# First-layer FFNs: gate/value pairs as seven half products instead of eight, and the second matrix in two passes

## The chip, the core and the metric

The kernel runs on one core of a Trainium2 chip. The time is the device time of one execution in microseconds (us), as the median of the runs shown. It multiplies in fp32 through TensorE: each operand is split into a high part that TensorE takes in one pass (fp32r) and a low part, the rest, and a product is three matmuls: high x high, low weight x high, high weight x low.

## The reference

Two "first" layers and two "second" layers on a sequence of 512 tokens, 1024 channels. A first layer has a SwiGLU FFN, a group of mixers, and a second SwiGLU FFN, each behind an RMS norm with a shift, scale and gate that come from a condition vector:

```python
def adaln_pre(h, g, shift, scale):
    return rms_norm(h, g) * (1 + scale) + shift

def swiglu(h, w13, w2):              # w13: 1024 x (2 * 2816), w2: 2816 x 1024
    a, b = jnp.split(h @ w13, 2, axis=-1)
    return (jax.nn.silu(a) * b) @ w2
```

The change is to `swiglu` in the first layers alone: 2 layers with 2 FFNs each, 4 in all.

## The kernel before

Activations lie channel by token: `xT` is 8 tiles of 128 channels x 512 tokens, `hH`/`hL` the split output of the norm, `gH`/`gL` the split gated product, 22 tiles of 128x512. A weight unit is 128 output channels with all their input tiles, 128x1024 (8 k tiles) in the first matrix and 128x1408 (11 k tiles, half of a column) in the second. A unit goes from `wR` (raw, by DMA on SyncE's queue) through ScalarE, which writes the high part `wH` (a copy that rounds, L1119), and VectorE, which writes the low part `wL = wR - wH` (L1687). There are two buffers, and a third one (`third`) for the openings.

An FFN is an opening, a loop and a second matrix:

- The norm works in two halves of 256 tokens. VectorE makes `hf` (L1822), ScalarE rounds it to `hH` (L1222), VectorE makes `hL` (L1828). Meanwhile `open_three` (PE, L2895) multiplies the first three units k by k in halves of 256 columns, and the fourth unit follows with 512.
- `up` (PE, L2927): the other 20 pairs of a gate and a value unit, each unit 8 k x 3 matmuls of 512 columns (`products`, L2890 to L2892). For each pair ScalarE takes the silu of the gate out of PSUM (L1169), VectorE multiplies it with the value (L1716), rounds (L1718) and takes the low part (L1720). In most pairs VectorE also makes two dots of 128x1024 against `cond` (L1662), for the shift, scale and gate of later norms; their weights `adaw` come by DMA.
- `down` (PE, L2949): 8 tiles of 22 k x 3 matmuls. VectorE adds each to `xT` with its gate (L1753); GpSimd squares it and adds up the squares for the next norm (`square_sum`, L2698 and L2701). The last tile is done in two halves of 256 columns (`last`, L2964 to L2966), and the mean square (L3008, L3011) is put between, so that root and norm of the next opening run beside the rest of it.

The order of each engine's instructions is written out by hand, with semaphores between engines (`w_hi`, `w_lo`, `w_used`, `sil`, `g_mul`, `x_new`). SyncE issues all DMAs in one order. In layer 0 the opening also holds the tables of the position bias: four matmuls and copies, and 32 small copies of GpSimd (`compressed_bias`, L2788).

## Time and profile before

| | |
|---|---|
| median of 3 runs | 3521.57 us (3520.69 to 3525.12) |
| span of the profiled execution | 3521.1 us |
| TensorE busy | 3406.2 us, 97% |
| TensorE weight loads | 2804.2 us, 80% |
| VectorE | 1994.7 us, 57% |
| ScalarE | 1164.4 us, 33% |
| GpSimd | 333.0 us, 9% |
| DMA | 386.77 MB, mean 110 GB/s |

All times are from one profiled execution, taken next to the runs; its span is 0.5 us below their median. In the lists a line is a line of the kernel, `PE` is TensorE's matmuls, `DVE` VectorE, `ACT` ScalarE, `POOL` GpSimd. `out<-in` names tiles without buffer numbers. A matmul's length in the timeline holds its way through the array, so back-to-back matmuls overlap: their rate is read from their starts.

### The profile page before, as it was taken

The page shows a single profiled execution, that of the slowest core. Times are in us where ns is not written, and L with a number is a line of the kernel's source. Part 1 is how long each engine was busy: PE and PEld are TensorE (multiplying, and loading weights), DVE is VectorE, ACT ScalarE, POOL GpSimd, SP SyncE. Part 2 cuts the span into 40 slices and gives each one's busy share as a digit, 9 for nine tenths or more (in the row PEclk, how much of TensorE's full clock was granted, in tenths as well). Part 3 has the DMA queues.
Part 4 walks back from the last instruction along what each step waited for, and adds up shares of the span by engine and source line. Part 5 has one row for each costly group of instructions (what it writes and reads, how often), then busy time and mean ns, then how long its engine had stood idle before and what let it go on. Part 6 is the DMA issues. An engine that isn't in the chain of part 4 may idle for free.

```text
span 3521.1 us, 49654 instructions
## 1 busy us (share of the span) xinstructions
PE 3406.2 (97%) x18508; PEld 2804.2 (80%) x18508; DVE 1994.7 (57%) x3164; ACT 1164.4 (33%) x1766; POOL 333.0 (9%) x293
## 2 busy tenths in 40 slices
PE   7999999989999999999998999999999999999999
PEld 6888877678888888887777888887788888688887
DVE  6763447666653566345766765446666625766642
ACT  4222334433221322234443322233443314443321
POOL 0000100141000000010014100011200011120002
PEclk9999999989999999999998999999999999999999
DMA  7653222103543355322210354321222332123232
GB/s 295 219 191 102 91 78 85 42 11 133 195 141 106 118 194 195 109 93 84 84 42 11 129 191 144 107 94 60 76 80 96 105 104 73 55 80 99 95 104 82
DMA packets 100835, 386.77 MB, mean 110 GB/s; under 512 B 11134, under 2 KB 12286, under 8 KB 99800
## 3 DMA queue, kind: packets, MB, share of 16 engines
q1 hardware_dynamic: 100696, 384.82, 32.0%
q8 instruction: 99, 1.62, 0.2%
q14 instruction: 40, 0.33, 0.0%
HBM read 382.65 MB, written 2.12 MB: 109 GB/s over the span
## 4 chain that ended last, share of the span: by engine, by line
PE 87%; DVE 7%; ACT 3%; issue 1%; DMA 1%; POOL 0%; SPq 0%; ACTq 0%; DVEq 0%; POOLq 0%
PE bank L2890 18%; PE bank L2892 18%; PE bank L2891 18%; PE bank L3016 4%; PE bank L3018 4%; PE bank L3017 4%; PE bank L2901 1%; PE bank L2902 1%; PE bank L2903 1%; PE bank L2966 1%; PE bank L2965 1%; PE bank L2964 1%; PE bank L3104 1%; PE bank L3627 1%; PE bank L3628 1%
## 5 line engine op out<-in xcount | busy, mean ns | idle before, releaser
L1119 ACT ACTIVATE wH<-wR 128x1024 fp32r<-128x1024 f32 (+2 forms) x378 | 428.9, 1135 | 1393.7 <-PE bank L2892 1305.5
L1687 DVE TENSOR_TENSOR wL<-wR,wH 128x1024 fp32r<-128x1024 f32 (+2 forms) x384 | 509.3, 1326 | 595.5 <-ACT wH L1119 591.0
L2890 PE MATMUL bank<-hH,wH 128*128 128x512 f32 x1920 | 747.8, 389 | 4.1 <-DVE wL L1687 4.1
L2892 PE MATMUL bank<-hL,wH 128*128 128x512 f32 x1920 | 747.6, 389 | 0.0
L2891 PE MATMUL bank<-hH,wL 128*128 128x512 f32 x1920 | 747.5, 389 | 0.0
L2890 PEld LDWEIGHTS bank<-hH,wH 128*128 128x128 f32 x1920 | 360.8, 188 | 79.7 <-DVE wL L1687 5.0
L2891 PEld LDWEIGHTS bank<-hH,wL 128*128 128x128 f32 x1920 | 360.8, 188 | 75.2
L2892 PEld LDWEIGHTS bank<-hL,wH 128*128 128x128 f32 x1920 | 360.6, 188 | 75.0
L2890 PE MATMUL bank<-gH,wH 128*128 128x512 f32 x924 | 359.4, 389 | 0.0
L2891 PE MATMUL bank<-gH,wL 128*128 128x512 f32 x924 | 359.4, 389 | 0.0
L2892 PE MATMUL bank<-gL,wH 128*128 128x512 f32 x924 | 359.4, 389 | 0.0
L3016 PE MATMUL bank<-hH,wH 128*128 128x512 f32 x672 | 285.8, 425 | 0.0
L3018 PE MATMUL bank<-hL,wH 128*128 128x512 f32 x672 | 266.2, 396 | 0.0
L3017 PE MATMUL bank<-hH,wL 128*128 128x512 f32 x672 | 265.3, 395 | 0.0
L2636 DVE SCALAR_TENSOR_TENSOR xn<-bank,par,xn 128x511 f32<-128x511 f32 (+1 forms) x176 | 131.5, 747 | 127.1 <-ACT xn L1604 115.7
L2891 PEld LDWEIGHTS bank<-gH,wL 128*128 128x128 f32 x924 | 173.4, 188 | 36.1
L2890 PEld LDWEIGHTS bank<-gH,wH 128*128 128x128 f32 x924 | 173.4, 188 | 36.1
L2892 PEld LDWEIGHTS bank<-gL,wH 128*128 128x128 f32 x924 | 173.4, 188 | 35.9
L1716 DVE TENSOR_TENSOR gf<-bank,sil 128x512 f32<-128x512 f32 x88 | 60.8, 691 | 244.9 <-PE bank L2892 241.8
L1662 DVE CUSTOM_DVE_ANT_0 adaw<-adaw,cond 128x1024 f32<-128x1024 f32 x144 | 170.3, 1220 | 0.0
L3016 PEld LDWEIGHTS bank<-hH,wH 128*128 128x128 f32 x672 | 128.3, 191 | 43.1 <-issue 20.6
L2698 POOL TENSOR_TENSOR sumsq<-xT 128x512 f32<-128x512 f32 x8 | 8.3, 1042 | 1611.6 <-DVE xT L1753 1582.7
(496 smaller groups left out, 5254.9 us busy)
## 6 DMA issues: line engine op xcount, KB each, us to landing
wR<-in_ffn_w SPq DMA_DIRECT2D x176, 512.0 KB, 3.4
adaw<-in_ada_w SPq DMA_DIRECT2D x144, 512.0 KB, 5.3
wR<-in_ffn_w SPq DMA_DIRECT2D x64, 704.0 KB, 4.0
wR<-in_w_up SPq DMA_DIRECT2D x88, 512.0 KB, 3.3
wR<-in_w_mix SPq DMA_DIRECT2D x76, 512.0 KB, 3.3
wR<-in_w_down SPq DMA_DIRECT2D x32, 704.0 KB, 4.0
wR<-in_w_in SPq DMA_DIRECT2D x40, 512.0 KB, 3.3
wR<-in_w_out SPq DMA_DIRECT2D x16, 512.0 KB, 3.3
```

Of the source, the lines that this page charges most:

```text
L1119: act.activation(wH[n][:, 0:tiles, :], wR[n][:, 0:tiles, :], ACT.Copy).then_inc(S.w_hi, 1)
L1662: return dve.tensor_tensor_reduce(w, w, cond[:, :], 1.0, 0.0, ALU.mult, ALU.add, dst)
L1687: dve.tensor_tensor(wL[n][:, 0:tiles, :], wR[n][:, 0:tiles, :], wH[n][:, 0:tiles, :].bitcast(F32), ALU.subtract).then_inc(S.w_lo, 1)
L1716: dve.tensor_tensor(gf[:, :], bank[b][:, :], sil[:, :], ALU.mult).then_inc(S.g_mul, 1)
L2636: dve.scalar_tensor_tensor(y, bank[b][:, 0:T - d], par[:, bass.ds(E_CW + 3 * (i + FT * half) + 2 - d, 1)], y, ALU.mult, ALU.add).then_inc( ...
L2890: pe.matmul(o, wH[n][:, k, :], rH[:, r, :], start=start and k == 0, stop=False)
L2891: pe.matmul(o, wL[n][:, k, :], rH[:, r, :], start=False, stop=False)
L2892: mm = pe.matmul(o, wH[n][:, k, :], rL[:, r, :], start=False, stop=stop and k == tiles - 1)
L2901: pe.matmul(o, wh[:, k, :], hH[:, k, c], start=k == 0, stop=False)
L3016: pe.matmul(o, wH[n][:, k, :], hH[:, k, :], start=k == 0, stop=False)
L3017: pe.matmul(o, wL[n][:, k, :], hH[:, k, :], start=False, stop=False)
L3018: mm = pe.matmul(o, wH[n][:, k, :], hL[:, k, :], start=False, stop=k == KT - 1)
```

## The change

In each first-layer FFN the first two gate/value pairs stay as they were. The other 20 are made one pair at a time as one product of a 2x2 block matrix. The weights of a pair are four blocks of 128 outputs x 512 inputs (gate or value, inputs 0 to 511 or 512 to 1023), h is four blocks of 512 inputs x 256 tokens. Eight block products become seven (Strassen, in Winograd's form), with sums of blocks ahead and sums of products behind:

- Weights: a pair comes as one DMA of 128x2048 (`RW`, two buffers). GpSimd makes four sums of 128x512 (`sums`). ScalarE rounds and VectorE takes low parts in three groups: 128x1536 (three raw blocks), 128x1024 and 128x1024 (the sums). The groups have one buffer each (`slots`), and group i of the next pair is written when its last product of this pair is done.
- h: the norm keeps its unrounded halves (`HB`, `wide`), GpSimd makes four block sums of 128x1024 once per FFN (`block_sum`), ScalarE and VectorE split them.
- Products: P1, P2, P4, P5, P6, P3, P7, each 4 k x 3 matmuls of 256 columns, each to a PSUM bank of its own (`turn`).
- Results: ScalarE copies P1 out of PSUM, VectorE makes seven sums of 128x256, each of one PSUM bank and one SBUF tile (`total`). ScalarE takes the silu of both halves, GpSimd multiplies with the value (`gated`, two of 128x256), ScalarE rounds, GpSimd takes the low part (`g_low`, 128x512).

The sums need space, so gated tiles are kept for half of the columns only (`gHc`, `gLc`, 11 tiles). The FFN runs in two chunks: 2 direct + 9 pairs, a pass of the second matrix over 11 k with its result added to `xT` (`x_mid`), then 11 pairs and a second pass over the other 11 k. In `down` a unit was half a column of the second matrix; it is now a tile of one pass, with an add to `xT` after each. The last tile is halved in the second pass only; the mean square stands 5 k into its second half, with 6 k behind it.

The dots are spread anew: one dot per turn for turns 1 to 8 of chunk A, in a layer's first FFN also for turns 1 to 10 of chunk B, the rest two by two in the passes of the second matrix. The dots of the first gate of layer 0, which had loads of their own, come in this stream. In layer 0 `compressed_bias` stands behind GpSimd's first sums and block sums and ahead of the sums of the turns. Semaphores of other parts are merged, with no change of order there. The numbers of the weights' layout on the host change to match.

The diff, cut to the turns and what feeds them:

```diff
+            # ScalarE
+            def chunk(f, q0, q1, u, half):
+                for q in range(q0, q1 + 1):
+                    keep_p1(f, q)
+                    if q > q0:
+                        g_high(f, q - 1)
+                    act.wait_ge(S.q_v, of(S.q_v, f, 7, n_sum("a_lo", q)))
+                    act.activation(sil[:, 0:W2], sil[:, 0:W2], ACT.Silu).then_inc(S.q_s, 1)
+                    act.wait_ge(S.q_p, of(S.q_p, f, 7, n_mult(4, q)))
+                    if q < q1:
+                        raw_in(f, q + 1)
+                        group1(f, q + 1)
+                        act.wait_ge(S.q_p, of(S.q_p, f, 7, n_mult(6, q)))
+                        group2(f, q + 1)
...
+                    act.wait_ge(S.q_v, of(S.q_v, f, 7, n_sum("a_hi", q)))
+                    act.activation(sil[:, W2:T], sil[:, W2:T], ACT.Silu).then_inc(S.q_s, 1)
+                    if q < q1:
+                        act.wait_ge(S.q_p, of(S.q_p, f, 7, n_mult(7, q)))
+                        group3(f, q + 1)
...
+            # VectorE
+            def chunk(f, q0, q1, u, half, c=None):
+                for q in range(q0, q1 + 1):
+                    dve.wait_ge(S.q_c, of(S.q_c, f, 1, q + 1))
+                    if q:
+                        dve.wait_ge(S.q_g, of(S.q_g, f, 2, 2 * q))
+                    total(f, q, "a_lo", 2, p1s, sil[:, 0:W2])
+                    if c is not None and q > q0 and q - q0 <= (10 if half else 8):
+                        dot(c + (q - q0 - 1) // 2, (q - q0 - 1) % 2)
+                    if q < q1:
+                        group1(f, q + 1)
...
+                    total(f, q, "u2", 6, p1s, u2s)
+                    summed(f, q, "u2")
+                    total(f, q, "x4", 4, u2s, x4s[:, :])
+                    total(f, q, "v", 5, u2s, vs[:, :])
+                    summed(f, q, "v")
+                    total(f, q, "a_hi", 3, vs[:, :], sil[:, W2:T])
+                    if q < q1:
+                        group2(f, q + 1)
+                    dve.wait_ge(S.g_lo, at(S.g_lo, FT * f + q + 2))
+                    total(f, q, "b_hi", 7, vs[:, :], gf[:, W2:T])
+                    total(f, q, "b_lo", 7, x4s[:, :], gf[:, 0:W2])
+                    if q < q1:
+                        group3(f, q + 1)
...
+            # GpSimd
+                    out, x, y, op = ((sA[:, 0:TT, :], a21, a22, ALU.add), (sA[:, TT:w, :], sA[:, 0:TT, :], a11, ALU.subtract),
+                                     (sB[:, 0:TT, :], a12, sA[:, TT:w, :], ALU.subtract), (sB[:, TT:w, :], a11, a21, ALU.subtract))[i]
...
+                    for q in range(q0, q1 + 1):
+                        if q > q0:
+                            gated(q - 1)
+                        if q < q1:
+                            pool.wait_ge(S.q_lo, of(S.q_lo, f, 3, 3 * q + 2))
+                            sums(q + 1, 0)
+                        if q > q0:
+                            g_low(q - 1)
+                        if q < q1:
+                            sums(q + 1, 1)
+                            pool.wait_ge(S.q_lo, of(S.q_lo, f, 3, 3 * q + 3))
+                            sums(q + 1, 2)
+                            sums(q + 1, 3)
...
+            # TensorE
+            def product(o, w, bh, bl):
+                wh, wl = w
+                for k in range(TT):
+                    pe.matmul(o, wh[:, k, :], bh(k), start=k == 0, stop=False)
+                    pe.matmul(o, wl[:, k, :], bh(k), start=False, stop=False)
+                    mm = pe.matmul(o, wh[:, k, :], bl(k), start=False, stop=k == TT - 1)
+                mm.then_inc(S.q_p, 1)
```

## Rows read from the trace of the kernel before

**Rows 1.** The page, part 4: shares of the chain that ended last
```profile
PE 87%; DVE 7%; ACT 3%; issue 1%; DMA 1%; POOL 0%; SPq 0%; ACTq 0%; DVEq 0%; POOLq 0%
```
**Rows 2.** Stretch table, first-layer FFN: stretch, length, busy us per engine, granted clock, DMA
```profile
850.00:1200.00 350.00, 350.00 (x1628) 293.45 (x1627) 167.36 (x228) 83.30 (x92) 15.92 (x13) 1.00 0.42 146
```
**Rows 3.** Timeline, TensorE, 512 columns: start, length, engine, line, operation (54 steps)
```profile
899.75 0.39 PE L2890 MATMUL bank<-hH,wH 128*128 128x512 f32 x1
...
911.99 0.39 PE L2890 MATMUL bank<-hH,wH 128*128 128x512 f32 x1
```
**Rows 4.** Timeline, TensorE, 256 columns, last tile of an FFN (86 steps)
```profile
395.81 0.28 PE L2964 MATMUL bank<-gH,wH 128*128 128x256 f32 x1
...
406.13 0.28 PE L2966 MATMUL bank<-gL,wH 128*128 128x256 f32 x1
```
**Rows 5.** Timeline, VectorE, two 128x1024 low parts back to back
```profile
36.49 1.22 DVE L1770 TENSOR_TENSOR third<-wR,third 128x1024 fp32r<-128x1024 f32 x1
37.63 1.22 DVE L1770 TENSOR_TENSOR wL<-wR,wH 128x1024 fp32r<-128x1024 f32 x1
```
**Rows 6.** Groups by shape, VectorE: count, busy us, mean ns, idle before
```profile
L1687 DVE TENSOR_TENSOR wL<-wR,wH 128x1024 fp32r<-128x1024 f32 x278 | 341.7, 1229 | 130.5 <-ACT wH L1119 125.9 <-ACT wH L1144 4.3 <-DVE gate L2368 0.2
...
L1716 DVE TENSOR_TENSOR gf<-bank,sil 128x512 f32<-128x512 f32 x88 | 60.8, 691 | 244.9 <-PE bank L2892 241.8 <-PE bank L2924 3.2
```
**Rows 7.** Groups by shape, GpSimd
```profile
L2830 POOL TENSOR_TENSOR pm<-pm,COS 128x512 f32<-128x512 f32 x16 | 20.6, 1285 | 151.1 <-PE bank L3565 151.1
...
L2727 POOL TENSOR_TENSOR hf<-pm 128x512 f32<-128x512 f32 x8 | 8.3, 1042 | 205.2 <-DVE pm L2157 205.2
...
L2751 POOL TENSOR_TENSOR OQ<-OD 128x1024 f32<-128x1024 f32 x2 | 3.8, 1895 | 80.3 <-ACT OD L1411 80.3
```
**Rows 8.** Groups by shape, ScalarE
```profile
L1119 ACT ACTIVATE wH<-wR 128x1024 fp32r<-128x1024 f32 x272 | 287.8, 1058 | 825.7 <-PE bank L2892 755.7 <-PE bank L3018 28.5 <-PE bank L2924 13.3
```
**Rows 9.** DMA issues: tile, queue, count, KB each, median us to landing
```profile
adag<-in_ada_first SPq DMA_DIRECT2D x3, 1024.0 KB, 7.3
```
**Rows 10.** Timeline, GpSimd and VectorE where both read two SBUF tiles
```profile
704.97 0.67 DVE L2218 TENSOR_TENSOR PP<-NN,LM 128x512 f32<-128x512 f32 x1
...
705.39 3.04 POOL L2769 TENSOR_TENSOR TMP<-NN,LM 128x512 f32<-128x512 f32 x2
...
705.67 1.64 DVE L2221 SCALAR_TENSOR_TENSOR PP<-PP,cst 128x512 f32<-128x512 f32 x1
...
707.23 1.75 DVE L2218 TENSOR_TENSOR PP<-NN,LM 128x512 f32<-128x512 f32 x1
```
**Rows 11.** Timeline, the same on a 128x1024 low part, and on a PSUM input
```profile
2548.95 1.22 DVE L1770 TENSOR_TENSOR third<-wR,third 128x1024 fp32r<-128x1024 f32 x1
...
2549.18 1.89 POOL L2698 TENSOR_TENSOR rstd<-xT 128x512 f32<-128x512 f32 x1 [5.31 <-DVE xT L2623]
...
2551.14 1.30 POOL L2701 TENSOR_TENSOR sumsq<-sumsq,rstd 128x512 f32<-128x512 f32 x1
...
2551.43 0.75 DVE L2623 SCALAR_TENSOR_TENSOR xT<-bank,gate,xT 128x512 f32<-128x512 f32 x1 [1.27 <-PE bank L3629]
```
**Rows 12.** Timeline, opening of an FFN: norm's second half, fifth unit
```profile
841.72 0.87 DVE L1822 SCALAR_TENSOR_TENSOR hf<-xT,modA,rstd 128x256 f32<-128x256 f32 x2
...
858.95 0.39 PE L2890 MATMUL bank<-hH,wH 128*128 128x512 f32 x1
```
**Rows 13.** Timeline, GpSimd: the compressed bias of layer 0
```profile
63.07 5.44 POOL L2788 COPY cb<-cskew 128x16 f32<-128x16 f32 x32 [62.63 <-DMA cskew<-bias_by_distance_up]
```
**Rows 14.** Timeline, TensorE: mean square, and first matmul of the next opening
```profile
406.25 0.60 PE L3008 MATMUL bank<-sumsq,cst 128*128 128x256 f32 x2
...
411.07 0.28 PE L2901 MATMUL bank<-hH,third 128*128 128x256 f32 x1
```
**Rows 15.** Stretch table, TensorE alone in the mixers: busy us (count), granted clock, DMA
```profile
728.00:736.00 8.00, 7.21 (x222) 1.00 0.01 2
704.00:712.00 8.00, 3.14 (x12) 0.64 0.00 0
```

More of the change, by code:

```diff
@@ L566, in build, with weights @@
         gL = place("gL", [P, FT, T], F32R)
+        o_wr = top[0]
         wR = [place(f"wR{i}", [P, KH, P]) for i in range(2)]
-        wH = [place(f"wH{i}", [P, KH, P], F32R) for i in range(2)]
-        wL = [place(f"wL{i}", [P, KH, P], F32R) for i in range(2)]
+        WT = 4 * P
+        w_hl = [place(f"w{n}", [P, 31, P], F32R) for n in ("H", "L")]
+        def weights(tile, tiles):
+            return [w[:, tile:tile + tiles, :] for w in w_hl]
+        wH, wL = zip(weights(0, KH), weights(12, KH))
+        third = weights(23, KT)
+        tail = weights(20, KH)
+        slots = [weights(4 * i, TT) for i in range(7)]
+        G1 = weights(0, 3 * TT)
+        G2 = weights(12, 2 * TT)
+        G3 = weights(20, 2 * TT)
         o_ex = [top[0]]
@@ L573, in build @@
         YC = place("YC", [P, 2, H * HD])
-        third = [place(f"third{i}", [P, KT, P], F32R) for i in range(2)]
         W3 = ((wH[0], wL[0]), (wH[1], wL[1]), third)
@@ L1052, in stream_ada @@
-                with sp.Fori(3 if start else 1, turns // 2) as i:
-                    for e in range(2):
-                        turn(2 * i + e, e, True)
-                with sp.Fori(turns, FT - 1) as i:
-                    turn(i, 0, False)
-                turn(FT - 1, 0, False)
+                sp.wait_ge(S.h_lo, at(S.h_lo, 2 * KT * (n + 1)))
+                sp.wait_ge(S.t_s, at(S.t_s, 4 * f + 4))
+                pair(f, 1, wq, l)
+                columns(c, l, False)
+                c += 1
@@ new lines, in columns, with group1, group2 @@
+            def columns(c):
+                for j in range(2):
+                    dot(c, j)
+            def group1(f, q):
+                dve.wait_ge(S.q_hi, of(S.q_hi, f, 3, 3 * q + 1))
+                dve.tensor_tensor(G1[1], RW[kind(q)][:, 0:3 * TT, :], G1[0].bitcast(F32), ALU.subtract).then_inc(S.q_lo, 1)
+            def group2(f, q):
+                dve.wait_ge(S.q_hi, of(S.q_hi, f, 3, 3 * q + 2))
+                dve.tensor_tensor(G2[1], sA[:, :, :], G2[0].bitcast(F32), ALU.subtract).then_inc(S.q_lo, 1)
@@ L1743, in up @@
-                with dve.Fori(4 if start else 1, turns // 2) as i:
-                    for e in range(2):
-                        turn(2 * i + e, KT)
-                        columns(2 * i + e, e)
-                dve.wait_ge(S.ada_done, at(S.ada_done, done + turns))
-                with dve.Fori(turns, FT - 1) as i:
-                    turn(i, KT)
-                turn(FT - 1, next_tiles)
-            def add_to_x(m, b, sub):
+                    dve.wait_ge(S.g_hi, at(S.g_hi, FT * f + i + 1))
@@ new lines, in ffn @@
+                gates()
+                for m in range(KT):
+                    if m == KT - 1:
+                        group1(f, Q_A)
+                        group2(f, Q_A)
+                        columns((ADA_DN1, ADA_DN2)[f] + m)
+                    dve.wait_ge(S.w_used, at(S.w_used, udn + m + 1))
+                    add_to_x(m, 2 + m % 2, sub, S.x_mid)
+                    if m + 2 < KT:
+                        down_low(udn, m + 2, 0)
+                    if m < KT - 1:
+                        columns((ADA_DN1, ADA_DN2)[f] + m)
@@ new lines, in ffn @@
+                group3(f, Q_A)
+                u = udn + KT
+                chunk(f, Q_A, NQ - 1, u, 1, None if f else ADA_UPB)
+                for m in range(KT - 1):
+                    dve.wait_ge(S.w_used, at(S.w_used, u + m + 1))
+                    add_to_x(m, 2 + m % 2, sub)
+                    if m + 2 < KT:
+                        down_low(u, m + 2, 1)
+                    if f == 0 and m < ADA_UP2 - ADA_FAR:
+                        columns(ADA_FAR + m)
+                    if rest and m < 4:
+                        rest(m)
@@ L2943, in up, with ffn @@
+            def ffn(f, ubase, udn, xbase, n, ss, between=None, late=False, start=False):
+                open_three(ubase, n, late, not start)
                 if between:
                     between()
-                gate_unit(1, bank[3][:, :])
-                with pe.Fori(2, FT) as i:
-                    turn(i)
+                pe.wait_ge(S.w_lo, at(S.w_lo, ubase + 4))
+                products_third(bank[3][:, :])
+                if between:
+                    pe.wait_ge(S.bm_set, H)
+                chunk(f, 0, Q_A, udn, 0, S.x_mid, KT * f)
+                chunk(f, Q_A, Q_B, udn + KT, 1, S.x_new, xbase, ss)
@@ L3476, in layer1 @@
                 warm(WARM)
-                up(U_UP2, FT, 2, late=True)
                 def next_layer():
```

731 lines of the change are left out of this document (504 added, 227 removed).

## The prediction

> **What bounds the kernel now.** First the page's chain [rows 1]: TensorE carries 87% of the chain that ended last, the next engine 7%. Then the stretch table of one first-layer FFN [rows 2]: in 850 to 1200 TensorE is busy 350.0 of 350 us at full clock, VectorE 167, ScalarE 83, GpSimd 16, and no wait of TensorE's is left to remove. So only TensorE's work counts here now, and the other engines have idle time. The question is whether they still have it when work is given to them.
>
> **What TensorE saves.** From 899.75 to 911.99 there are 54 steps between matmuls of 512 columns: 0.2267 us each [rows 3]. From 395.81 to 406.13 there are 86 steps of 256 columns: 0.1200 us [rows 4]. Half the columns cost more than half the time. A pair is 48 matmuls of 512 before (2 units, 8 k, 3 split products): 10.88 us. After it is 7 products of 4 k, 3 split products, 256 columns: 84 x 0.12 = 10.08 us. That is 0.80 us less, times 80 pairs (20 in each of 4 FFNs): 64 us, if TensorE sets the pace.
> The second matrix keeps its 528 matmuls of 512 columns per FFN; its last tile is halved over 11 k instead of 22, which saves 66 x 0.12 - 33 x 0.2267 = 0.44 us per FFN.
> The Trainium skill (TensorE: Matmul & The Clock Gate, Back-to-back issue gap) gives 262 cycles for 256 columns and 518 for 512, that is 109 and 216 ns at 2.4 GHz. By it the saving would be 1.19 us a pair, 95 us in all; the rows show 120 and 227 ns, and the rows decide.
>
> **What the other engines get per pair.** Rates first. Back-to-back VectorE steps: 1.14 us for 128x1024 with two SBUF inputs (36.49 to 37.63) [rows 5]; so 1.67 for 128x1536 (half as much again, less a start of 0.09 counted once: a single one shows 1.229 [rows 6]). An add of 256 columns from PSUM is about 0.34, half of the 0.69 for 512 [rows 6]. GpSimd: 1.285 us for 128x512 with two different inputs, 1.042 for a square, 1.895 for a 1024 square [rows 7].
> VectorE per pair: low parts of the weight groups 1.67 + 1.14 + 1.14 = 3.95, seven PSUM adds 2.4, and in 26 of the 40 pairs of a layer one modulation dot of 1.14. Together 7.5 us, inside 10.08. ScalarE: 1.5 + 1.06 + 1.06 of weights (1.06 for 128x1024 [rows 8]) and four small ones: 5.5 us. GpSimd: four weight sums, the gate's two half products and its low part: 6.6 to 7.5 us. Each fits alone. DMA bytes do not change; a pair comes as one transfer of 1 MB, which the nearest row lands in 7.3 us [rows 9], two turns ahead. These I cost at nothing.
>
> **What they can't do together.** Where GpSimd's 128x512 operations and VectorE's with two SBUF inputs meet, each stands still for the other's whole length [rows 10]. VectorE's L2218 takes 0.67 alone (704.97). L2221, of the same size, starts at 705.67 and takes 1.64; the next L2218 starts at 707.23 and takes 1.75; GpSimd's two take 3.04. From one end to the next (707.31 to 708.98) is some 1.69 with the step between them, for one of each: 0.60 of VectorE (half of 1.14 and a start) and so 1.09 of GpSimd. The same at 2548.95 [rows 11]: GpSimd's square takes 1.89 instead of 1.04 behind a 128x1024 low part, while VectorE's add from PSUM at 2551.43 takes 0.75 in the middle of a GpSimd sum, which takes its 1.30. So the two share one door to SBUF, taken for a whole instruction; VectorE's operations with a PSUM input don't need it.
> The Trainium skill says so too (SBUF — State Buffer, SBUF: two separate sides): the pair of ports shared by VectorE and GpSimd is an exclusive lock, held for the instruction, for VectorE operations with two SBUF inputs. It speaks against this change, and by it the sum comes out as from the rows.
> Before the change GpSimd works 16 us in an FFN, so the door is free. After it, per pair: GpSimd 5 x 1.09 + 2 x 0.57 (half of it, rounded up) = 6.6, VectorE 3.95: 10.55 us, and 11.7 with a dot. That is over TensorE's 10.08, and over the old 10.88 where there is a dot. I walked a turn through in program order with these lengths and the 0.1 us that GpSimd takes to start after what releases it: the door then stands idle 0.5 to 1.0 us a turn (GpSimd waiting for a sum of its own, or for VectorE's PSUM adds), so a turn takes **12.2 us with a dot, 11.6 without**.
> The operands are ready ahead at a chunk's start and no sums are made at its end. So of a chunk's 9 or 11 turns the door sets about 6 and 7; the first ones cost 10.1 to 12.7 by the same walk, the last 10.1. Chunk A, with dots: 12.7 + 10.8 + 6 x 12.2 + 10.1 = 106.8. Chunk B with dots (first FFN of a layer): 10.1 + 10.1 + 11.4 + 7 x 12.2 + 10.1 = 127.1, without (second FFN) 122.1. Against 20 x 10.88 = 217.6: **+16.3 and +11.3 us** per FFN.
>
> **Openings.** At present the first four units need the norm, and 3.1 + 5.8 + 2.9 + 5.4 = 17.2 us pass from the norm's second half (841.72) to the fifth unit (858.95) [rows 12]. The change puts through the door in that time: 16 norm operations at 0.87 the two 7.0, two first weight sums 2.2, four block sums of 128x1024 at about 2.1 (above 1.9, the square) 8.4, three low parts of third and blocks 3.4, one in four pieces 1.6, the gate's 0.6, the first weight group 1.7, two more weight sums 2.2: 27.1 us. So the first product starts about **9.9 us** late. Minus the 0.44: FFN +25.8 and +20.8. If GpSimd's sums waited instead of the norm, half of it would be hidden (5 us); that end is in the range.
> In layer 0 the compressed bias (5.44 us of GpSimd [rows 13]) moves behind the first sums and ahead of the turns' own: +5 (0 to 5.4).
>
> **The end of each FFN.** At present the mean square starts at 406.25 and the next opening at 411.07 [rows 14]: 0.7 us of its own and 4.1 us of the last tile cover the chain of root, norm and split that the opening waits for. After the change 6 k of 256 columns follow, 2.2 us. The cover is 1.9 us shorter: up to +1.9 each. A part comes back, since VectorE no longer waits for its own low part in the norms of the FFNs. I take +1 each, **+4** in all (0 to 7).
>
> **Sum.** 2 x (25.8 + 20.8) + 5 + 4 = +102 us on the profiled execution's 3521.1, which is 3623; the median of the runs is only 0.5 above that execution: **3624 us**.
>
> **Rivals.**
> 1. The door is no bound: the two engines overlap in these operations, or GpSimd's waits fall where VectorE adds from PSUM. Then TensorE runs through: 4 x (-16 - 0.44) = -66, openings of 2 to 3 us each +10, the ends +4: -52, **3470 us**. For it: every engine alone fits, and in all turns VectorE has 2.4 us of PSUM adds for GpSimd to slip past. Against: 10.55 us of door time don't fit in 10.08 however they are ordered; it needs GpSimd's door time under 1.0 per 512 columns, and the rows give 1.09. It decides if door time per turn falls under 10.1.
> 2. The custom dot doesn't take the door (no row has it beside GpSimd): every turn 11.6. The 15 or so dot turns of the door in a layer's first FFN and 6 in its second lose 0.6 each: 2 x 21 x 0.6 less, +77, **3598 us**.
> 3. The clock. TensorE will stand 2 us in each turn. In 728 to 736, busy 7.2 of 8 us in short pieces, it was granted the full 2.4 GHz; in 704 to 712, busy 3.1 of 8, 0.64 [rows 15]. A turn is busy 10.1 of 12.2, like the first, so I expect full clock in turns. If it falls to 1.2 GHz after the openings' 9 us gap, each loses some 3 us: +12, **3636 us**. If it fell in every turn, a product would take twice as long and the turn 20 us; I give that 2%.
>
> **How the numbers follow.** Forecast (door sets the turn) 0.70, rival 2 0.08, rival 3 0.08, rival 1 0.14. Bounds of the forecast: GpSimd's 512 columns at 1.0 and VectorE's steps 0.07 shorter give turns of 11.4 and 10.8 by the same walk and +45 us (3566); GpSimd at 1.18 (1.285 less the 0.1 in which it only starts), gives 12.7 and 11.7 and +135 us (3657). The range 3560 to 3665 holds these, rivals 2 and 3, and leaves out rival 1. Faster by over 0.2% (7 us, about what can be told from no change here) 0.14; within 0.02; slower 0.84.
>
> **What would show it.** The GpSimd sums at more than 1.285 us on average, and VectorE's low parts of weights over 1.67 and 1.14; starts of a turn 12.2 us apart in chunk A and 11.6 in chunk B of the second FFNs; TensorE idle before the first product of a turn, released by VectorE's first low part; 256-column steps still 0.12. Wrong is the forecast if TensorE is busy throughout the FFNs, if low parts keep their 1.23 us beside GpSimd, or if turns with and without a dot are equal.

## The result and the profile after

The kernel after takes 3644.2 us (median of 4 runs, 3640.3 to 3648.4), against 3523.4 us (4 runs, 3520.7 to 3525.6) beside it: ratio 1.0345, 95% interval 1.0331 to 1.036, so 121 us slower. The forecast was 3624, in a range of 3560 to 3665. The profiled execution's span went from 3521.1 to 3638.4 us, +117.3.

First the page: busy time and share by engine, then the shares of the chain that ended last (before: [rows 1]).
```profile
PE 3399.1 (93%) x21256; PEld 2919.6 (80%) x21256; DVE 2420.0 (67%) x3617; ACT 1388.4 (38%) x2134; POOL 1320.0 (36%) x869
...
PE 57%; POOL 16%; DVE 14%; ACT 6%; issue 5%; DMA 2%; SPq 0%; POOLq 0%; ACTq 0%; DVEq 0%
```
TensorE is 93% busy but carries only 57% of the chain; 16% are GpSimd's, which had none. The table of what TensorE waited for (us in total, times, longest) has one large new row, and the stretch of an FFN that answers to [rows 2] shows the same from the engines' side: TensorE is busy 325 of 350 us and GpSimd 239 where it was 16.
```profile
PE bank L3314 <- DVE wL L1918: 97.3, 75, 4.8
```
```profile
890.00:1240.00 350.00, 325.06 (x2174) 300.60 (x2173) 236.49 (x306) 132.00 (x170) 238.57 (x149) 0.98 0.37 128
1112.00:1180.00 68.00, 62.56 (x504) 61.09 (x504) 41.89 (x62) 30.77 (x42) 67.14 (x43) 1.00 0.25 88
```
The second row is six turns of chunk B of a second FFN, without dots: GpSimd is busy 67.1 of 68 us. Much of that is not its own work but waiting at the door, which the profile counts as busy, as the groups by shape show (count, busy us, mean ns, idle before):
```profile
L3111 POOL TENSOR_TENSOR sum<-RW 128x512 f32<-128x512 f32 x160 | 333.6, 2085 | 289.0 <-DVE wL L1944 138.9 <-DVE wL L2062 88.0 <-DVE wL L1923 62.0
L3111 POOL TENSOR_TENSOR sum<-sum,RW 128x512 f32<-128x512 f32 x80 | 208.8, 2610 | 1.3
L3111 POOL TENSOR_TENSOR sum<-RW,sum 128x512 f32<-128x512 f32 x80 | 107.5, 1344 | 47.9 <-DVE wL L1928 26.5 <-DVE wL L1944 12.2
L3124 POOL TENSOR_TENSOR gLc<-gf,gHc 128x512 fp32r<-128x512 f32 x80 | 154.8, 1935 | 11.9 <-ACT gHc L1296 11.9
...
L1918 DVE TENSOR_TENSOR wL<-RW,wH 128x1536 fp32r<-128x1536 f32 x80 | 170.4, 2130 | 48.6 <-ACT wH L1275 48.4
L1923 DVE TENSOR_TENSOR wL<-sum,wH 128x1024 fp32r<-128x1024 f32 x80 | 105.0, 1312 | 47.9 <-ACT wH L1280 47.9
L1928 DVE TENSOR_TENSOR wL<-sum,wH 128x1024 fp32r<-128x1024 f32 x80 | 107.4, 1342 | 107.8 <-ACT wH L1285 107.8
L1872 DVE CUSTOM_DVE_ANT_0 adaw<-adaw,cond 128x1024 f32<-128x1024 f32 x144 | 241.2, 1691 | 27.6 <-DMA adaw<-in_ada_w 27.0
L1908 DVE COPY mod<-acc 128x2 f32<-128x2 f32 x72 | 35.3, 490 | 2.5
L1933 DVE TENSOR_TENSOR vs<-bank,rstd 128x256 f32<-128x256 f32 x80 | 33.1, 414 | 0.0
```
GpSimd's 128x512 operation alone is 1285 ns [rows 7]; here it is 2085, 2610, 1344 and 1935. VectorE's 128x1536 low part is 2130 where 1.67 us was expected, the dot 1691 against 1220 alone. The add of 128x256 from PSUM stays at 414, as it does in the runs below that take either engine's share away (414 in both). Together they are a lock seen from both sides.

One turn without a dot, GpSimd's and VectorE's timeline (start, length, idle time before in brackets), and TensorE's first matmul of this turn and of the next:
```profile
1110.47 2.80 POOL L3111 TENSOR_TENSOR sum<-sum,RW 128x512 f32<-128x512 f32 x1
1113.41 1.30 POOL L3111 TENSOR_TENSOR sum<-RW,sum 128x512 f32<-128x512 f32 x1
1114.67 2.28 POOL L3111 TENSOR_TENSOR sum<-RW 128x512 f32<-128x512 f32 x1
1116.92 1.43 POOL L3118 TENSOR_TENSOR gf<-gf,sil 128x256 f32<-128x256 f32 x2
1118.31 2.27 POOL L3111 TENSOR_TENSOR sum<-RW 128x512 f32<-128x512 f32 x1
1120.53 1.30 POOL L3124 TENSOR_TENSOR gLc<-gf,gHc 128x512 fp32r<-128x512 f32 x1
1121.80 2.79 POOL L3111 TENSOR_TENSOR sum<-sum,RW 128x512 f32<-128x512 f32 x1
...
1110.30 1.82 DVE L1918 TENSOR_TENSOR wL<-RW,wH 128x1536 fp32r<-128x1536 f32 x1 [1.86 <-ACT wH L1275]
1114.46 1.34 DVE L1923 TENSOR_TENSOR wL<-sum,wH 128x1024 fp32r<-128x1024 f32 x1 [0.75 <-ACT wH L1280]
1118.13 1.29 DVE L1928 TENSOR_TENSOR wL<-sum,wH 128x1024 fp32r<-128x1024 f32 x1 [1.67 <-ACT wH L1285]
1121.62 1.83 DVE L1918 TENSOR_TENSOR wL<-RW,wH 128x1536 fp32r<-128x1536 f32 x1 [1.86 <-ACT wH L1275]
...
1112.26 0.38 PE L3314 MATMUL bank<-hH,wH 128*128 128x256 f32 x1 [0.89 <-DVE wL L1918]
1123.59 0.38 PE L3314 MATMUL bank<-hH,wH 128*128 128x256 f32 x1 [0.90 <-DVE wL L1918]
```
From the GpSimd sum at 1110.47 to the one at 1121.80 are 11.33 us, and it never rests: its second sum lasts 2.80 because VectorE holds the door from 1110.30 to about 1112.1 for the first low part, the fourth 2.28 because of the low part at 1114.46. TensorE's turn goes from 1112.26 to 1123.59, 11.33 us as well, with 0.9 us of idle time that VectorE's low part ends.

Reading TensorE's timeline at each turn's first matmul gives the account by stage (us; the second FFN of layer 0, and for the last row the first FFN of layer 1):

| stage | before | after | forecast |
|---|---|---|---|
| norm's second half to the fifth unit or first product | 17.2 | 26.9 | 27.1 |
| chunk A, 9 turns (with dots) | 97.9 | 108.5 | 106.8 |
| chunk B, 11 turns, no dots | 119.7 | 123.4 | 122.1 |
| both passes of the second matrix, ends | 123.3 | 125.4 | 123.9 |
| chunk B with dots (first FFNs) | 119.7 | 132.6 | 127.1 |

(Before, 9 and 11 pairs of 10.88 us. A chunk's last turn is counted to the first matmul of the second matrix. The 5 us between the mean square and the norm's second half stand in no row.) The second FFN of layer 0 as a whole, between its mean square and the next, went from 363.55 to 389.30 (+25.8), the first FFN of layer 1 from 363.8 to 399.2 (+35.4).

### The profile page after: what moved, and what is told of

Read it like the earlier page. It is cut to its first block, busy times and chain, and to the rows that moved or that the text cites. A ratio compares the mean times of both kernels' runs of the same rounds, so it can differ in the third digit from the quotient of the medians.

```text
span 3638.4 us, 55528 instructions
## 1 busy us (share of the span) xinstructions
PE 3399.1 (93%) x21256; PEld 2919.6 (80%) x21256; DVE 2420.0 (67%) x3617; ACT 1388.4 (38%) x2134; POOL 1320.0 (36%) x869
## 4 chain that ended last, share of the span: by engine, by line
PE 57%; POOL 16%; DVE 14%; ACT 6%; issue 5%; DMA 2%; SPq 0%; POOLq 0%; ACTq 0%; DVEq 0%
POOL sum L3111 9%; PE bank L3272 6%; PE bank L3271 6%; PE bank L3273 6%; PE bank L3488 4%; PE bank L3490 4%; PE bank L3489 4%; PE bank L3368 4%; PE bank L3370 4%; PE bank L3369 4%; POOL gLc L3124 3%; POOL gf L3118 2%; DVE adaw L1872 2%; ACT wH L1280 1%; DVE hf L2117 1%
## 5 line engine op out<-in xcount | busy, mean ns | idle before, releaser
L3111 POOL TENSOR_TENSOR sum<-RW 128x512 f32<-128x512 f32 x160 | 333.6, 2085 | 289.0 <-DVE wL L1944 138.9
L3314 PE MATMUL bank<-hH,wH 128*128 128x256 f32 x960 | 297.8, 310 | 102.4 <-DVE wL L1918 97.3
L3314 PE MATMUL bank<-tH,wH 128*128 128x256 f32 x1280 | 363.1, 284 | 0.0
L3315 PE MATMUL bank<-tH,wL 128*128 128x256 f32 x1280 | 362.7, 283 | 0.0
L3316 PE MATMUL bank<-tL,wH 128*128 128x256 f32 x1280 | 362.0, 283 | 0.0
L1891 DVE TENSOR_TENSOR wL<-wR,wH 128x1024 fp32r<-128x1024 f32 (+2 forms) x160 | 209.7, 1311 | 205.4 <-ACT wH L1231 205.3
L3314 PEld LDWEIGHTS bank<-hH,wH 128*128 128x128 f32 x960 | 196.3, 204 | 123.6 <-issue 78.6
L3488 PE MATMUL bank<-hH,wH 128*128 128x512 f32 x672 | 285.1, 424 | 0.0
L3490 PE MATMUL bank<-hL,wH 128*128 128x512 f32 x672 | 265.6, 395 | 0.0
L3489 PE MATMUL bank<-hH,wL 128*128 128x512 f32 x672 | 264.6, 394 | 0.0
L1872 DVE CUSTOM_DVE_ANT_0 adaw<-adaw,cond 128x1024 f32<-128x1024 f32 x144 | 241.2, 1691 | 27.6 <-DMA adaw<-in_ada_w 27.0
L3271 PE MATMUL bank<-hH,wH 128*128 128x512 f32 x640 | 249.9, 390 | 4.1 <-DVE wL L1891 4.1
L3272 PE MATMUL bank<-hH,wL 128*128 128x512 f32 x640 | 249.9, 390 | 0.0
L3273 PE MATMUL bank<-hL,wH 128*128 128x512 f32 x640 | 249.9, 390 | 0.0
```

Source lines behind the costliest of these rows:

```text
L3111: pool.tensor_tensor(out, x, y, op).then_inc(S.q_sum, 1)
L3271: pe.matmul(o, wH[n][:, k, :], rH[:, r, :], start=start and k == 0, stop=False)
L3272: pe.matmul(o, wL[n][:, k, :], rH[:, r, :], start=False, stop=False)
L3273: mm = pe.matmul(o, wH[n][:, k, :], rL[:, r, :], start=False, stop=stop and k == tiles - 1)
L3314: pe.matmul(o, wh[:, k, :], bh(k), start=k == 0, stop=False)
L3315: pe.matmul(o, wl[:, k, :], bh(k), start=False, stop=False)
```

## Experiments

Times are to be read against the kernel after, 3644 (its four runs lie between 3640 and 3648, so a few us mean nothing by themselves); the first four are one run each, the others medians of two. Turn lengths are read from TensorE's timeline as above, or from ScalarE's copy of the first product where it shows the turn more plainly.

**The three engines in a turn, one at a time.** GpSimd's sums cut:
```diff
+                    if q not in (0, Q_A):
+                        out, x, y = (v[:, :, 0:8] for v in (out, x, y))
                     pool.tensor_tensor(out, x, y, op).then_inc(S.q_sum, 1)
```


> Undoes GpSimd's share: inside the turns its four sums of quarters (L3111 in the kernel after) work on 8 of 128 columns of each tile, so they leave most of the sum undone; waits, order and everything else stay. Shared door (theory): GpSimd's demand per turn falls from 6.6 us to about 2 (one low part of 1.09 and two products), VectorE's low parts fall back to 1.67 and 1.14 us, the door needs 6 us a turn and TensorE's 84 steps of 0.12 = 10.08 us set the turn. 12.33 us turns lose 2.25 us, 11.32 us turns lose 1.24: per layer 26 steps x 2.25 + 10 x 1.24 = 71 us, both layers 142 us, 3644 -> about 3500 us. Rival (TensorE is slower than its 0.12 us steps say, through its clock or its waits for the seven results): turns stay above 12 us and the time stays within 20 us of 3644.

Measured 3511.8 us, 132 less (about 3500 us expected). All turns of all chunks are 10.08 us apart but each chunk's first ones. Eighty us of chunk B, with TensorE without a gap:
```profile
1045.00:1125.00 80.00, 80.00 (x669) 80.00 (x669) 56.84 (x80) 42.55 (x58) 45.60 (x56) 1.00 0.26 93
```
The first turn of chunk A still takes 12.24 us in the second FFN of layer 0, and nearly all of it is TensorE's: behind the opening's 4.8 us of idle time its first 24 steps take 5.0 us instead of 2.9 (granted clock 0.52 in 862 to 867), and nothing else is waited for. small_lows shows the same (12.23).

VectorE's low parts cut, GpSimd whole:
```diff
-                dve.tensor_tensor(G1[1], RW[kind(q)][:, 0:3 * TT, :], G1[0].bitcast(F32), ALU.subtract).then_inc(S.q_lo, 1)
+                low, raw, high = few(q, G1[1], RW[kind(q)][:, 0:3 * TT, :], G1[0])
+                dve.tensor_tensor(low, raw, high.bitcast(F32), ALU.subtract).then_inc(S.q_lo, 1)
```
(`few` takes 8 of 128 columns in all pairs but a chunk's first; the two other groups alike.)

> Takes VectorE's share of the door away and leaves GpSimd whole: inside the turns VectorE's three low parts of weights work on 8 of 128 columns of each tile (most of the low part is left undone). Shared door (theory): GpSimd's sums fall back from 2.09 us to 1.285 us or less, its seven instructions need about 7.8 us, less than TensorE's 10.08; turns come down to 10.1 to 10.3 us where there is no dot, to at most 11 with one, total about 3500 to 3540 us. Rival (GpSimd is too slow by itself, the door has no part in it): its sums stay at 2.09 us and the turns at 12.3 and 11.3 us, total within 20 us of 3644.

Measured 3508.3 us. GpSimd does just what it did, yet its groups by shape are shorter, and a stretch of ten turns in chunk B has TensorE without a gap:
```profile
L3118 POOL TENSOR_TENSOR sum<-RW 128x512 f32<-128x512 f32 x160 | 216.5, 1353 | 288.8 <-DVE wL L1951 139.9 <-DVE wL L2069 87.8 <-DVE wL L1929 61.1
L3131 POOL TENSOR_TENSOR gLc<-gf,gHc 128x512 fp32r<-128x512 f32 x80 | 109.3, 1366 | 11.9 <-ACT gHc L1296 11.9
```
```profile
1055.00:1155.00 100.00, 100.00 (x721) 95.03 (x721) 36.87 (x78) 43.25 (x54) 61.65 (x53) 1.00 0.30 103
```
The sum went from 2085 to 1353 ns, the gated low part from 1935 to 1366. So GpSimd isn't slow by itself; taking away either engine's share is enough. The rival of a GpSimd that is too slow falls.

The dots cut to 64 of 1024 columns:
```diff
-                dots(adaw[s + j][:, :], acc[:, c % 2, j:j + 1]).then_inc(S.ada_sum, 1)
+                w = adaw[s + j][:, 0:64]
+                dve.tensor_tensor_reduce(w, w, cond[:, 0:64], 1.0, 0.0, ALU.mult, ALU.add, acc[:, c % 2, j:j + 1]).then_inc(S.ada_sum, 1)
```


> Takes the dots out of the turns: every dot of the adaLN columns (L1872) works on 64 of its 1024 columns, so the modulation values are wrong; its loads, waits and the small copy behind it stay. Shared door that the dot takes too (theory): the 12.33 us turns become 11.3 like those of the second FFNs' second chunk; 8 steps in each first chunk and 10 in each second chunk of the first FFNs, 52 steps x 1.0 us = 52 us, 3644 -> about 3592 us. Rival (the dot needs no door, and the second chunks are quicker for another reason): under 10 us less.

Measured 3578.2 us, 66 less where 52 were expected. Turns of 12.33 became 11.36 (11.33 and 11.40 by turns). The other 14 us, by the stages: a dot behind each tile of the second matrix also held VectorE up at the seam between the chunks. The seam (the first pass of the second matrix, up to chunk B's first product) went from 61.35 to 59.98 us, and chunk B's first turn from 12.06 to 10.08.

A third of TensorE's work in the turns taken out:
```diff
-                    pe.matmul(o, wl[:, k, :], bh(k), start=False, stop=False)
-                    mm = pe.matmul(o, wh[:, k, :], bl(k), start=False, stop=k == TT - 1)
+                    mm = pe.matmul(o, wl[:, k, :], bh(k), start=False, stop=k == TT - 1)
```


> Takes a third of TensorE's work out of the turns: the seven half products leave out the product of the high weights with the low part of the input; the waits stay. Shared door (theory): TensorE's 6.7 us a turn instead of 10.08 change little, since the door's 10.6 to 11.7 us set the turn; turns stay within 0.3 us of 12.3 and 11.3, total 3620 to 3644 us. Rival (the turn is a chain in which TensorE's products stand with their full length, as the profile's chain, 57% TensorE, can be read): 3.4 us less a turn until the door binds, turns near 10.6 and 11.7 or less, total under 3600 us.

Measured 3639.3 us: 3.4 us less work in each of 80 turns, 269 us of TensorE, is worth 5, which one run can't tell from nothing. The turns say it better: 12.27 us with a dot, 11.29 without one. More than half of what TensorE was spared it waits, 193 and 72 us in place of the 97 of the kernel after:
```profile
PE bank L3314 <- DVE wL L1918: 193.2, 79, 4.8
PE bank L3314 <- DVE wL L1928: 72.2, 63, 2.9
```
Part of the rest went into slower matmuls: in 900 to 1000 the mean granted clock was 0.84, against 0.95 in the kernel after, and the turns were no longer for it. The 57% of TensorE in the chain of the kernel after were no bound of the turns.

**Sums moved to VectorE.** If only the door's demand counted, this had to pay, since VectorE holds it for a shorter time. A copy of the sum's code runs on VectorE; GpSimd's calls for these sums go, with a semaphore of their own for the first two:
```diff
+                    if q + 2 <= q1:
+                        for i in range(2):
+                            weight_sum(f, q + 2, i)
                     if q < q1:
                         group3(f, q + 1)
```
(This is vector_sums2, the first two sums; vector_sums3 and vector_sums4 move the others too.)

> Moves two of the four sums of quarters of each turn (the two that make the first of the two sum tiles) from GpSimd to VectorE, just ahead of its third low part; nothing is left out. Shared door (theory): a sum holds the door for about 1.09 us from GpSimd and about 0.65 us from VectorE, so the demand falls from 10.55 to 9.7 us a turn, with a dot from 11.8 to 10.9. Turns of 10.1 to 10.4 us without a dot and 11.2 with one in place of 11.32 and 12.33: 72 steps x 1.1 us = 79 us, 3644 -> about 3565 us. Rival (the turn is VectorE's own work and its waits in order, 67% busy over the span): 1.3 us more work for it makes the turns longer, 3644 -> 3700 us or more.

> Three of the four sums of each turn on VectorE, one stays on GpSimd. Shared door (theory): demand 9.2 us without a dot, 10.4 with one; VectorE's own work 8.8 and 10.2 us. Turns at TensorE's 10.1 us without a dot and 10.6 to 10.9 with one: 52 x 1.6 + 20 x 1.2 us = 107 us, 3644 -> about 3537 us. Rival (VectorE's work sets the turn): longer than with two sums moved.

> All four sums of each turn on VectorE; GpSimd keeps the gate's products and the low part of the gated tile. Shared door (theory): demand 8.8 us, 10.0 with a dot, no longer the bound; VectorE's own work is now 9.5 us, and 10.9 with a dot, and it takes the bound over in the turns with a dot: 10.1 us without one, about 11.1 with one, 52 x 1.2 + 20 x 1.2 us = 86 us, 3644 -> about 3558 us, so slower than with three moved. If it is quicker than with three, the door's demand and not VectorE's work was still the bound there.

Measured 3606.9, 3650.5 and 3643.6 us. Turns without and with a dot (the kernel after: 11.32, 12.33): 10.79 and 11.80 with two sums moved, 11.38 and 12.40 with three, 11.92 and 11.99 with four. Two moved sums gave half of what the door's demand promised. Four gave a turn that is neither the door's nor TensorE's, and that a dot lengthens by 0.07 us only. VectorE's timeline of vector_sums4 in a turn without a dot, the first low part, and at the end the third and the next turn's first total:
```profile
1121.13 1.76 DVE L1919 TENSOR_TENSOR wL<-RW,wH 128x1536 fp32r<-128x1536 f32 x1 [1.86 <-ACT wH L1276]
1129.64 1.21 DVE L1929 TENSOR_TENSOR wL<-sum,wH 128x1024 fp32r<-128x1024 f32 x1
1130.78 0.41 DVE L1950 TENSOR_TENSOR sil<-bank,rstd 128x256 f32<-128x256 f32 x1
```
VectorE works through from 1121.13 to 1131.19 and then stands still 1.86 us, in which ScalarE makes the high part that the next low part needs. 10.06 + 1.86 = 11.92. A dot stands in this gap by program order and so costs next to nothing. So it is VectorE's work (the part of it that waits for the door included), in its program order, plus the gap.

The two other kernels have the same gap, and the same sum holds in their turns without a dot: 8.93 + 1.86 = 10.79 with two sums and 9.52 + 1.86 = 11.38 with three. So from two sums on each further one costs VectorE its own 0.60 us, and that is why three are slower than two. With two or three a dot in the gap still costs 1.0 us: there GpSimd has a sum left, it takes the door behind the dot, and VectorE's copy or low part that follows waits (1.13 us for a copy with three sums, 2.82 for the 128x1536 low part with two). With four nothing of GpSimd's stands there. That four came out 7 us below three comes of this, and is no sign of the door's demand in the turns without a dot.

What the gap is made of stands in ScalarE's timeline of the same turn:
```profile
1131.22 0.42 ACT L1313 ACTIVATE sil<-sil 128x256 f32<-128x256 f32 x1 [1.39 <-DVE sil L1950]
1131.55 1.47 ACT L1276 ACTIVATE wH<-RW 128x1536 fp32r<-128x1536 f32 x1
```
By its program order ScalarE rounds the next weights only behind the silu of VectorE's first total. It had been idle for 1.39 us just before, and the other condition for the rounding, TensorE's third product, was met some 3.5 us before the silu began (the three products start at 1123.02 and take 36 x 0.12 = 4.3 us). So the rounding ahead of the silu looks like the direct way to close the gap; no run tried it.

**The gap filled.**
```diff
+                    if q < q1:
+                        for i in range(2):
+                            weight_sum(f, q + 1, i)
                     if q < q1:
                         group1(f, q + 1)
```
(gap_sums2; gap_sums4 has the two other sums where vector_sums4 has them.)

> Two sums on VectorE as in vector_sums2, but issued a turn later, right behind the turn's first total (and its dot), where VectorE stood idle for 1.86 us in every turn of vector_sums2 until ScalarE had the first group's high part. Theory now (a turn costs VectorE the door's delays and its own work, plus the part of this 1.86 us that nothing fills): 1.3 us of sums move from the loaded part into the idle stretch, the 10.79 us turns fall to TensorE's 10.1 to 10.3 us; with a dot (1.2 us, which fills most of the idle stretch already) 11.8 falls by 0.3 to 0.6 us only. 20 x 0.6 + 52 x 0.45 = 35 us off 3607, about 3572 us. Rival (the door's demand alone, whatever the place): demand is the same as in vector_sums2, so no change, 3607 us.

> All four sums on VectorE as in vector_sums4, two of them in the idle stretch behind the first total. Theory (VectorE's work plus unfilled idle stretch): vector_sums4's turns were 11.92 us with and without a dot, because the dot fell into the idle 1.86 us; with 1.3 us of sums in it the turns without a dot fall to about 10.6 us and those with one to about 11.8, since dot and sums together overfill it: 20 x 1.3 + 52 x 0.15 = 34 us off 3643, about 3609 us. Rival (door alone): no change, and turns with and without a dot still equal.

Measured 3619.7 and 3651.7 us: both slower than with the sums in their first place. Without a dot the four-sum turn did fall, 11.92 to 11.31, half of what was expected; with two sums 10.79 became 10.87. With dots they rose to 12.59 and 12.15. VectorE in gap_sums4, from the last low part of a turn on:
```profile
1126.51 1.71 DVE L1929 TENSOR_TENSOR wL<-sum,wH 128x1024 fp32r<-128x1024 f32 x1
1128.91 0.43 DVE L1950 TENSOR_TENSOR sil<-bank,rstd 128x256 f32<-128x256 f32 x1 [0.69 <-issue]
1129.25 0.68 DVE L1945 TENSOR_TENSOR sum<-RW 128x512 f32<-128x512 f32 x1
1129.97 1.68 DVE L1945 TENSOR_TENSOR sum<-sum,RW 128x512 f32<-128x512 f32 x1
1131.57 1.75 DVE L1919 TENSOR_TENSOR wL<-RW,wH 128x1536 fp32r<-128x1536 f32 x1
```
and GpSimd's beside it:
```profile
1126.40 2.41 POOL L3141 TENSOR_TENSOR gf<-gf,sil 128x256 f32<-128x256 f32 x2 [6.62 <-DVE gf L1950]
1129.56 1.53 POOL L3147 TENSOR_TENSOR gLc<-gf,gHc 128x512 fp32r<-128x512 f32 x1 [0.74 <-ACT gHc L1297]
```
VectorE's last low part takes 1.71 behind GpSimd's gate products. The next turn's first total waits 0.69 us; the trace calls it issue, but the program lets it write the gate's tile only when these products have read it, and they end at 1128.81. The moved sum at 1129.97 takes 1.68 behind GpSimd's low part at 1129.56, where the one before it takes 0.68. The gap of 1.86 us is filled, but the sums no longer stand between VectorE's other work and GpSimd's gate products: the last low part meets them (1.71 for 1.21, +0.5) and the next total waits for them (+0.69). The two sums themselves are held up in either place, 1.18 + 1.11 us in vector_sums4 and 0.68 + 1.68 here (+0.07). Together this is the 0.6 us by which the turn without a dot fell. The theory of "work plus gap" was too simple: it left out where in the turn GpSimd comes to the door. The turns with a dot were not taken apart in this way.

**The opening.** ScalarE's and VectorE's first group ahead of the block sums' low parts:
```diff
-                sum_low(0)
                 pair_out(0, 1)
+                group1(f, 0)
+                sum_low(0)
                 sum_low(1)
                 sum_low(2)
-                group1(f, 0)
```
(ScalarE alike; TensorE's wait for all four block sums is split, three for product 4, the fourth for product 7.)

> The opening alone: ScalarE and VectorE split the first group of the first pair's weights ahead of the low parts of the block sums (there behind them), and TensorE's third product waits for three of the four block sums' low parts, its last for the fourth. Theory (9.9 us of each opening are the block sums' chain through the door, and the first product stands behind low parts that it doesn't need): in the second FFN of the first layer TensorE's idle time of 4.8 us before its first product of turns goes, and the following turn keeps its start up to 2 us of it; 3 to 5 us in each of four FFNs, 3644 -> 3624 to 3632 us. Rival (the first low part is late since its weights come late): no change.

Measured 3641.6 us, no difference that the runs can tell from 3644. TensorE, in the kernel after and then reordered, each row a matmul with the idle time before it:
```profile
897.99 0.58 PE L3314 MATMUL bank<-hH,wH 128*128 128x256 f32 x1 [4.81 <-DVE wL L1918]
```
```profile
899.78 0.39 PE L3314 MATMUL bank<-tH,wH 128*128 128x256 f32 x1 [1.69 <-DVE tL L1983]
908.05 0.39 PE L3314 MATMUL bank<-hH,wH 128*128 128x256 f32 x1 [3.69 <-DVE wL L1928]
```
The wait of 4.81 us is gone and the first product starts 27.1 us behind the mean square's last step (L3483 in the kernel after) instead of 32.1. But 1.69 and 3.69 us are waited for in the same turn, at a block sum's low part (L1983) and at the third group's (L1928): from the mean square to the end of chunk A 140.8 us against 140.6. VectorE has some 20 us of work nearly in a row at this place (887.72 to 908.33 here), and TensorE meets the same end of it in either order.

So the block sums themselves had to go to price them:
```diff
-                    pool.tensor_tensor(tF[t][:, :, :], x[:, :, :], y[:, :, :], ALU.subtract).then_inc(S.t_s, 1)
+                    pool.tensor_tensor(tF[t][:, :, 0:8], x[:, :, 0:8], y[:, :, 0:8], ALU.subtract).then_inc(S.t_s, 1)
```


> Prices the opening by itself: GpSimd's four sums of the input's blocks, ScalarE's high parts and VectorE's low parts of them work on 8 of 256 columns, and TensorE takes the first block of the input where it would take a sum, so four of the seven products are of the wrong input; waits and the turns' own work stay. Theory: GpSimd's 11.0 us and VectorE's 10.0 us in the opening go, TensorE's first product starts right behind the fourth opening product (26.9 us behind the second mean square instead of 32.1) and the first turn lasts about 10.2 instead of 12.6 us, 7 to 8 us in each of four FFNs; the turns behind keep 12.33 and 11.32 us. 3644 -> 3610 to 3616 us. Rival (as reordering the opening showed, what is gained there is only waited for later, since the turns behind are bound by the door): the whole FFN shortens by under 3 us, 3632 us or more.

Measured 3604.0 us, 40 less, and more than the 28 to 34 expected. The second FFN of layer 0 lasts 378.5 us instead of 389.3, the first product comes 23.2 us behind the mean square (before the change 22.7 to the fifth unit, and 26.9 were expected), the first turn takes 10.37 us, and the turns behind it keep 12.33 and 11.32. The rival, that turns bound by the door swallow the gain, falls.

> Does what small_lows and small_blocks do together (most of the turns' low parts and the block sums are left undone). It closes the account: with turns at 10.08 us in all four FFNs and no block sums in the openings only the chunks' seams and the compressed bias are left of the change's costs. 3508 - 4 x 7.3 = about 3479 us. If the opening's price shows here and not in small_blocks, the opening is dear only where TensorE sets the turns, and behind it in the kernel after the door's turns swallow it.

Measured 3475.8 us (3479 expected), ratio 0.987 to before (0.984 to 0.990). The same FFN takes 350.7 us, 12.9 less than before the change. The page's chain and the stretch table:
```profile
PE 82%; DVE 10%; ACT 3%; DMA 2%; issue 2%; POOL 0%; SPq 0%; ACTq 0%; DVEq 0%; POOLq 0%
```
```profile
855.00:905.00 50.00, 50.00 (x419) 50.00 (x418) 34.40 (x63) 27.79 (x38) 40.81 (x34) 1.00 0.42 147
```
It leaves work out, so this is a price and not a faster kernel: without the door in the turns and without the openings the change is what it looks like on TensorE alone, near the 3470 us of the first rival.

## Why the prediction was right, and where its terms were off

- **The bound.** Right: the door's demand passes TensorE's 10.08 us a turn. Taking away either side of it (small_sums, small_lows) brought 10.08 back in all turns but each chunk's first one or two; a third of TensorE's work taken out did next to nothing (two_products). The Trainium skill (SBUF — State Buffer, SBUF: two separate sides) calls the shared pair of ports an exclusive lock; the trace agrees, 2085 ns beside VectorE's low parts and 1353 without them.
- **TensorE's steps.** Right: with nothing else in the way, 84 matmuls of 256 columns take 10.08 us a turn (small_sums, small_lows, small_both). The 262 cycles of the Trainium skill (TensorE: Matmul & The Clock Gate, Back-to-back issue gap) are its figure for the gap of an isolated matmul, which by the same section of the Trainium skill under-counts at small sizes in a stream with weight loads; an estimate from that figure is 84 x 109 ns = 9.2 us. The runs decide for the rows of before.
- **The turns: right in kind, under-sized in sum.** Forecast +16.3 and +11.3 us an FFN, measured +23.4 and +14.2, which is 20 of the 117 us. Chunk A's first steps came as walked (12.56 and 10.72 against 12.7 and 10.8). The turns with a dot are 12.33 for 12.2, those without 11.32 for 11.6. The failed step is "the operands are ready ahead at a chunk's start and no sums are made at its end". In the first FFNs chunk B's first turn took 12.06 instead of 10.1, its second 10.72 instead of 10.1 and its third 12.36 instead of 11.4; in the second FFNs the first took 12.06 too, but the third 10.92. small_dots shows the first turn to be the dots of the passes between the chunks, behind which VectorE came late (10.08 without them). The last turn of each chunk took 11.0 to 11.3 instead of 10.1: its products some 10.3, and then TensorE waited for the low part of the second matrix's first unit (0.77 us at the end of chunk A in the second FFN of layer 0). In small_sums and small_lows this wait is gone (10.08). The walk's own sum for chunk B without dots is 10.1 + 10.1 + 11.4 + 7 x 11.6 + 10.1 = 122.9, and not the 122.1 that the forecast has; this is 1.6 us in all.
- **The dot takes the door.** Rival 2 fell: 1691 ns instead of 1220, and 1.0 us a turn in small_dots. The small copy behind every second dot was costed at nothing. It takes 490 ns in the groups above, against this row of before:
```profile
L1705 DVE COPY mod<-acc 128x2 f32<-128x2 f32 x14 | 2.4, 168 | 0.5
```
- **Openings.** Forecast 9.9 us, 27.1 from the norm's second half; measured 26.9 against 17.2, 9.7 more, in three of them. small_blocks gave 40 us for four. The opening of layer 0's first FFN took 28.9 us from the norm's second half, only 2.0 more than the others, and 21.0 before the change, so it cost 7.9. The +5 for the compressed bias does not show: its copies (72.5 to 83.6) fall for the most part where GpSimd stands idle in the other openings (6.26 and, one pair of sums later, 4.24 us in the second FFN of layer 0), and chunk A behind it takes 108.3 us like the others' 108.4. All four together: 37 us, forecast 44.6.
- **Ends.** Forecast +1 and -0.44 an FFN; what is neither opening (from the norm's second half) nor turns grew by some 2 us an FFN, 8.5 in all. Of this 1.4 to 2.0 each is the seam between the chunks, which small_dots took away (59.98 us in all four FFNs). The last 0.5 us or so fits the forecast for the end, but no run shows it by itself.
- **Cancelling.** Turns +20, ends +6, openings -8, and -3.7 in layer 0's mixers: the sum missed by 15 us of 117, its terms by more, so that 3624 came this near to 3644 is in part luck. The mixers' part has nothing to do with the change. TensorE has the same 2933 matmuls from one FFN to the next there, and is busy throughout the stretch in which most of the difference arises, but at another granted clock. The same work, first before and then after:
```profile
454.00:461.00 7.00, 7.00 (x16) 0.54 0.00 0
```
```profile
487.00:494.00 7.00, 7.00 (x27) 0.80 0.01 2
```
Over all runs on record this stretch of layer 0 took 419.6 to 427.2 us (423.3 before, 419.6 after). A sum that is read from one profiled execution carries such a few us with it.
- **The clock.** Rival 3's mechanism is there: in 895 to 905, with 4.8 us of idle time just before the first product (897.99), the mean granted clock was 0.66, and it is 1.00 again in the next 10 us:
```profile
885.00:895.00 10.00, 8.18 (x47) 6.88 (x45) 8.63 (x9) 5.94 (x11) 7.89 (x4) 1.00 0.42 158
895.00:905.00 10.00, 7.01 (x41) 7.01 (x42) 9.04 (x11) 5.35 (x9) 2.79 (x2) 0.66 0.41 158
905.00:915.00 10.00, 9.86 (x83) 9.66 (x82) 8.07 (x11) 4.57 (x7) 3.93 (x4) 1.00 0.29 105
```
The first product's and the second's 24 steps took 5.07 us instead of 2.9, most of them 0.21 each and so at the lower level of 1.2 GHz. It cost nothing that can be seen: this turn took 12.56 us where 12.7 had been walked at full clock, and TensorE still waited 0.3 us at its end for VectorE's low part, which the door had made late. But there is little between the two. In small_sums and small_lows the door no longer sets this turn, and it takes 12.24 and 12.23 us for 10.08: there the clock is the price, some 2.1 us an FFN. In small_blocks the idle time ahead of the first product is gone, the granted clock is 1.00 from 875 to 890, and the turn takes 10.37.

## What to carry to other kernels

Before work is given to an idle GpSimd, add up the time in which it and VectorE both read SBUF, per turn of the loop, and compare it with the engine that sets the pace; the busy shares of 67% and 36% tell nothing of it, and each engine fitted alone. The sign of such a lock in a profile is that both engines' operations grow and those from PSUM don't. Shifting work between the two ends of a lock pays less than the demand says, because it also shifts where in the turn they meet. Where an engine's program has a gap of fixed length in every turn, look first at what the engine that it waits for does just before. Taking away a wait at an opening whose engines are full only names the next one; shrink the work itself to learn its price.

None of the complete versions that were run is faster than the kernel before; the best is vector_sums2 at 3607 us, 1.024 times before (1.021 to 1.027).

## What the runs showed of the hardware

- A custom reduction of VectorE with two SBUF inputs is held up beside GpSimd like a plain one (1220 to 1691 ns on average), and so is a copy of two columns (168 to 490 ns on average; 169 ns where it meets nothing, 1140 at the longest).
- Thirty-two GpSimd copies of 128x16 elements, 5.44 us in a row before [rows 13], took 11.06 us where VectorE works beside them. A small operation can wait for the door as long as a large one. One tile's instructions, shortest, median and longest in ns:
```profile
L3096 POOL COPY cb<-cskew x32: 202/210/1814, 72.5 to 83.4; 128x16 f32<-128x16 f32 x32
```
- The rule holds per meeting, not per instruction: GpSimd's third sum (1344 ns on average; 1113.41 in the timeline above) comes when VectorE adds from PSUM or waits, and nearly keeps the 1285 it takes alone.
- Turns with and without a dot can be equal: where the order of an engine's program leaves a gap for another engine's answer (1.86 us here), other work fits in: in vector_sums4 a dot that took 1.97 us in it cost 0.07 us a turn on average.
